# Down stage of a product-key expert layer: which token tiles have their gates scattered, placed by one-hot products, or gathered

## The chip, the cores and the metric

The kernel runs on one core of a Trainium2 chip. The metric is the device time of one launch in microseconds. The core has TensorE (PE), VectorE (DVE), ScalarE (ACT), GpSimd (POOL) and SyncE (SP), each with its own list of instructions that runs in order; they meet in semaphores.

## The reference

One decoder layer over 1024 tokens of width 1024: a mixing sublayer (dilated attention and gated DeltaNet), a norm, a product-key expert sublayer (PEER) and a norm. The change is in PEER:

```python
q = (t @ w_query).reshape(T, PEER_HEADS, 2, PEER_HALF)
s = jnp.einsum('thpc,hpkc->thpk', q, sub_keys).astype(f32)
top_s, top_i = lax.top_k(s, PEER_TOPK)
...
best_s, best_j = lax.top_k(cand_s, PEER_TOPK)
experts = jnp.take_along_axis(cand_i, best_j, axis=-1)
gate = jax.nn.softmax(best_s, axis=-1)
...
act = jax.nn.gelu(jnp.einsum('pd,phkd->phk', xb, expert_down[eb]).astype(f32), approximate=False)
return jnp.einsum('phk,phkd->pd', (gb * act).astype(x.dtype), expert_up[eb])
```

Each token chooses 8 x 16 = 128 of 128 x 128 = 16384 experts, with a gate for each. An expert has one row of `expert_down` and one of `expert_up`.

## The kernel before

Stages run one after the other, with a barrier between: projection, attention, DeltaNet, merge, output projection with norm, scores, then `stage_down_and_route` (the down stage) and `stage_up`.

The 1024 tokens are eight tiles of 128. Six tiles are dense (`DENSE`): the down stage multiplies them with all 16384 experts, in 128 chunks of 128 experts, and stores the gelu as `act`; `stage_up` multiplies `act` by a gate matrix `W` in DRAM, which is zero but for the 128 chosen experts of each token, and by `expert_up`. Two tiles are gathered (`GATHERED`): for them only the chosen rows are read, `expert_down` rows in the down stage and `expert_up` rows in the up stage.

The gates of a dense tile come into `W` in one of two ways. A scattered tile (`SCATTERED`) has its zeroes written in the DeltaNet stage (`blank`, L650) and then has its gates added by 128 indirect DMAs of GpSimd (`scatter`, L1708), one for each choice, of 128 gates each. A placed tile (`PLACED`) has 32 groups of four one-hot products: DVE makes `r_oi` (L1742), ScalarE makes `r_oj` (L1636, L1639), PE multiplies them into `r_psw` (L1923), ScalarE copies that to `r_W` (L1645), and eight DMAs of 1 MB store it (L1587).

Work of the down stage by chunk `c`, each engine in its own loop:

- PE: 48 products of `x1` with the chunk (`L1935`, high and low parts of the weights and of `x1`), two halves of 24. In a chunk that belongs to a placed tile (`pair_in`) two groups of one-hot products follow, one behind each half. A placed tile takes 16 chunks, from four chunks behind its routing; two chunks before them PE transposes its routes (`turn`, L1912).
- ScalarE: gelu of the chunk (`r_act`, L1671) when its products are done, the high part `r_dh` of the weights of chunk `c + 3` (L1618), and its part of the one-hots.
- DVE: the low part `r_dl` of chunk `c + 2` (`split_d`, L1733; three buffers), one-hots, one of the 14 pieces of the routing of a tile (`topk`), the dot products of gathered rows (`dot_row`, L1750), and at the end the one-hots for the first half of chunk `c + 1`. Pieces 12 and 13 are the longest; behind piece 13 the tile is routed. Routed are tiles 0 to 7 in chunks 6, 13, 27, 41, 55, 69, 83 and 97.
- GpSimd: the scatters of the chunk and then the gathers for its dots (L1699): for a dot `k` the row `k + 4` is gathered into the buffer that the dot set free (four buffers, `NGB`). If a group of 16 scatters begins in the chunk, these scatters come behind the gathers, and the first waits for all 16 before.
- SP: loads of weights, stores of `act` and of `W`.

Lists worked out when the kernel is built say how many scatters and dots a chunk has. Before: tile 0's scatters in chunks 7 to 55 (two or three a chunk), tile 4's in 56 to 121 (two), dots in chunks 28 to 83 (two or three) and 84 to 126 (three). Groups of placed tiles are chunks 17 to 32, 45 to 60, 73 to 88 and 101 to 116. All of a kernel's DMAs of GpSimd stand in one list with each other, so a gather waits behind the scatters ahead of it:

```python
for c in range(PK):
    fresh = next((x for x in scatters[c] if x % TOP == 0), scatters[c].stop)
    for x in range(scatters[c].start, fresh):
        scatter(SCATTERED[x // P], x % P)
    if c == first_dots:
        for k in range(NGB):
            gather(k)
    for k in dots[c]:
        if k + NGB < NG2 * P:
            gather(k + NGB)
```

Of the kernel before, what the change touches and what calls it, by code (L numbers as in the profile page):

```python
# [9 lines left out]
ALU = mybir.AluOpType  # L10
# [18 lines left out]
N_BR = 2 * KD  # L29
N_IN = N_ATT + N_DN + N_GB + N_BR  # L30
PH, PK, TOP = 8, 128, 16
SCATTERED = (0, 4)
GATHERED = (2, 6)
PLACED = (1, 3, 5, 7)
DENSE = SCATTERED + PLACED
ORDER = GATHERED + DENSE
ND, NG2 = len(DENSE), len(GATHERED)
# [1435 lines left out]
def stage_down_and_route(nc, g):  # L1473
# [33 lines left out]
        n = stop - first  # L1507
        return [0] * first + [count * (k + 1) // n - count * k // n for k in range(n)]

    split_at = routed_in[SCATTERED[1]] + 1  # L1510
    scatters = spread(evenly(routed_in[SCATTERED[0]] + 1, split_at, P) + evenly(0, PK - 6 - split_at, P))
    scatters += [range(NS * P, NS * P)] * (PK - len(scatters))
    middle = routed_in[GATHERED[1]] + 1
    first_dots = routed_in[GATHERED[0]] + 1
    dots = spread(evenly(first_dots, middle, P) + evenly(0, PK - 1 - middle, P) + [0])
    last_dot = [next(c for c, part in enumerate(dots) if P * (n + 1) - 1 in part) for n in range(NG2)]
    ring = [(k + 1 + k // P) % NGB for k in range(NG2 * P)]
    x_slot = [n * (P + 1) % NGB for n in range(NG2)]
# [8 lines left out]
    with ExitStack() as ctx:  # L1527
        def sb(name, shape, dt=F32):
# [1 line left out]

        sem = ctx.enter_context(stage_semaphores(nc, "r",
            "ld_d0 ld_d1 ld_d2 ld_st ld_c ld_x st_W d_lo gelu st_a0 st_a1 st_used W d_hi shifted exp oi oj off turned rt "
            "d_mm w_mm eq picked summed pieces passed chain zsum routed dots x_in gelu_g coef", landed="ld_g0 ld_g1 ld_g2 ld_g3 put0 put1"))
        xh, xl = g.x1h, g.x1l
        draw = [sb(f"r_draw{u}", [P, KD, P]) for u in range(DEEP)]
        dh = [sb(f"r_dh{u}", [P, KD, P], F32R) for u in range(DEEP)]
# [152 lines left out]
        @block.gpsimd  # L1689
        def _(pool):  # L1690
            def gather(k):
                n, u = k // P, ring[k]
                if k % P == 0:
                    pool.wait_ge(sem("routed"), START + GATHERED[n] + 1)
                if k % P == NGB - 1:
                    pool.wait_ge(sem("x_in"), START + n + 1)
                elif k >= NGB:
                    pool.wait_ge(sem("dots"), START + k - NGB + (2 if 0 <= k - P < NGB - 1 else 1))
                nc.gpsimd.indirect_dma_start(out=rows[u][:], out_offset=None, in_=g.down_rows,  # L1699
                                             in_offset=bass.IndirectOffsetOnAxis(ap=g.ids[:, n, k % P:k % P + 1], axis=0)).then_inc(sem(f"ld_g{u}"), 16)  # L1700

            def scatter(t, e):
                n = SCATTERED.index(t)
                if e == 0:
                    pool.wait_ge(sem("routed"), START + t + 1)
                elif e % TOP == 0:
                    pool.wait_ge(sem(f"put{n}"), 16 * e)
                nc.gpsimd.indirect_dma_start(out=cells, out_offset=bass.IndirectOffsetOnAxis(ap=place[:, n, e:e + 1], axis=0),  # L1708
                                             in_=put[:, n, e:e + 1], in_offset=None, compute_op=ALU.add).then_inc(sem(f"put{n}"), 16)

            cells = g.W.rearrange("j p (t o) -> (j p t) o", o=1)
            for c in range(PK):
# [9 lines that stand above are left out]
                for x in range(fresh, scatters[c].stop):  # L1722
                    scatter(SCATTERED[x // P], x % P)
            for n in range(NS):
                pool.wait_ge(sem(f"put{n}"), 16 * P)

        @block.vector
        def _(dve):
# [33 lines left out]
            def topk(t, piece):  # L1762
# [54 lines left out]
                elif piece == 6:  # L1817
                    before()
                    for h in range(PH):
                        done = nc.vector.max(best[:, h, 0:8], cand[:, h])  # L1820
                elif piece == 7:
                    before()
                    for h in range(PH):
                        done = nc.vector.max_index(flat[:, h, 0:8], best[:, h, 0:8], cand[:, h])
                elif piece == 8:
                    before()
                    for h in range(PH):
                        done = nc.vector.match_replace(out=cand[:, h], in_to_replace=best[:, h, 0:8], in_values=cand[:, h], imm_value=GONE)
                elif piece == 9:
                    before()  # L1830
                    for h in range(PH):
                        done = nc.vector.max(best[:, h, 8:16], cand[:, h])
                elif piece == 10:
                    before()
                    for h in range(PH):
                        nc.vector.max_index(flat[:, h, 8:16], best[:, h, 8:16], cand[:, h])

                    dve.wait_ge(sem("turned"), START + sum(d < t for d in PLACED))
                    nc.vector.tensor_tensor(route[:, 2], best[:], best[:, :, 0:1].broadcast_to([P, PH, TOP]), ALU.subtract).then_inc(sem("shifted"), 1)
                    dve.wait_ge(sem("shifted"), START + t + 1)  # L1840
                    dve.sem_inc(sem("pieces"), 1)
                elif piece == 11:

                    before()
                    nc.vector.tensor_copy(flatf[:], flat[:])
                    chained(nc.vector.scalar_tensor_tensor(comb[:], keyf[:, :, 0, :], 64.0, starts8, ALU.mult, ALU.add), 1)
                    nc.vector.tensor_copy(rise[:, :, 0:1], comb[:, :, 0:1])
                    chained(nc.vector.tensor_tensor(rise[:, :, 1:], comb[:, :, 1:], comb[:, :, 0:TOP - 1], ALU.subtract), 2)
                    dve.wait_ge(sem("exp"), START + t + 1)
                    nc.vector.tensor_reduce(zsum[:], route[:, 2], AX.X, ALU.add).then_inc(sem("zsum"), 1)  # L1850
                    dve.wait_ge(sem("zsum"), START + 2 * t + 1)
                    nc.vector.reciprocal(zsum[:], zsum[:]).then_inc(sem("zsum"), 1)
                    dve.wait_ge(sem("zsum"), START + 2 * t + 2)
                    done = nc.vector.tensor_tensor(route[:, 2], route[:, 2], zsum[:].unsqueeze(2).broadcast_to([P, PH, TOP]), ALU.mult)
                elif piece == 12:
                    before()
                    picked(0, flatf[:], starts16, ALU.is_ge, rise[:])
                    chained(nc.vector.tensor_copy(code[:], route[:, 0]), 3)
                    nc.vector.tensor_scalar(low[:], code[:], 63, None, ALU.bitwise_and)
                    chained(nc.vector.tensor_scalar(high[:], code[:], 6, None, ALU.logical_shift_right), 4)  # L1860
                    nc.vector.tensor_copy(route[:, 0], high[:])
                    chained(nc.vector.tensor_copy(comb[:], low[:]), 5)
                    chained(nc.vector.tensor_tensor(flatf[:], flatf[:], comb[:], ALU.subtract), 6)
                    dve.sem_inc(sem("pieces"), 1)
                elif piece == 13:
                    before()
                    picked(1, flatf[:], ranks16, ALU.is_equal, keyf[:, :, 1, :])
                    if t not in PLACED:
                        both = comb[:].rearrange("p h a -> p (h a)")
                        r0, r1, r2 = (route[:, x].rearrange("p h a -> p (h a)") for x in range(3))  # L1870
                        chained(nc.vector.scalar_tensor_tensor(both, r1, float(PK), r0, ALU.mult, ALU.add), 7)
                        if t in GATHERED:
                            n = GATHERED.index(t)
                            nc.vector.tensor_copy(gate[:, n], r2)
                            chained(nc.vector.tensor_copy(g.ids[:, n], both), 8)
                        else:
                            n = SCATTERED.index(t)
                            nc.vector.tensor_copy(put[:, n], r2)
                            chained(nc.vector.tensor_scalar(place[:, n], both, float(TD), tokens[:, n:n + 1], ALU.mult, ALU.add), 8)
                    else:  # L1880
                        dve.sem_inc(sem("chain"), CHAIN - 6)
                    dve.sem_inc(sem("routed"), 1)  # L1882
                    dve.sem_inc(sem("pieces"), 1)
# [425 lines left out]
```

## Time and profile before

| | us |
|---|---|
| time, median of 3 (4306.22 to 4308.96) | 4306.57 |
| the profiled execution | 4310.81 |
| its span | 4309.0 |
| down stage, first product to last gelu | 1960.0 to 3189.3 |
| up stage, first product | 3208.3 |

| engine | busy us | share of the span |
|---|---|---|
| PE | 3957.7 | 92% |
| DVE | 2586.9 | 60% |
| ScalarE | 1367.3 | 32% |
| GpSimd | 1702.3 | 40% |

Busy times are sums over the whole span and say nothing of one stage. A row of a group gives busy time, the mean ns of one instruction and the idle time of its engine just before, with what ended it. GpSimd is counted busy while it makes the descriptors of an indirect DMA, not while the data move.

### The profile page before, as it was taken

What the parts mean: (1) busy time and instruction counts of PE and PEld (TensorE: products, weight loads), DVE (VectorE), ACT (ScalarE), POOL (GpSimd) and SP (SyncE); (2) the same over time, 40 slices, a digit from 0 to 9 for tenths busy, and PEclk for the clock granted to TensorE, in tenths of its full rate; (3) what the DMA queues carried; (4) which work ended last, traced back from release to release, by engine and by line L of the source; (5) the groups of instructions that cost most, each with busy time, mean ns of one, the idle gap of its engine ahead of it and who ended that gap; (6) DMA issues with size and microseconds to landing.
All of it is one profiled execution on the core that took longest, in us unless ns stands there. A gap on an engine that the chain in (4) does not pass through costs nothing. (4 is left out here: it accounts for less than half of the span.)

```text
span 4309.0 us, 61280 instructions
## 1 busy us (share of the span) xinstructions
PE 3957.7 (92%) x21744; PEld 3573.4 (83%) x21744; DVE 2586.9 (60%) x5114; ACT 1367.3 (32%) x2139; POOL 1702.3 (40%) x1159
## 2 busy tenths in 40 slices
PE   9999994996888788998999999999988999999996
PEld 7888884886888666998999999999976888888885
DVE  2154102554555334116777888886648888898888
ACT  2133221652222211112472644635512222222220
POOL 0000003624444004000727656566626555555556
PEclk9999996997999899999999999999999999999998
DMA  3223224642222322223549779698888888888884
GB/s 132 97 88 106 94 86 129 160 109 71 76 75 84 138 95 94 88 68 129 136 139 318 231 227 299 201 331 278 262 315 289 289 291 290 285 290 298 280 289 185
DMA packets 390923, 801.82 MB, mean 186 GB/s; under 512 B 65265, under 2 KB 204401, under 8 KB 389745
## 3 DMA queue, kind: packets, MB, share of 16 engines
q1 hardware_dynamic: 280176, 531.25, 36.9%
q0 software_dynamic: 110592, 268.62, 19.9%
q8 instruction: 85, 1.39, 0.1%
q14 instruction: 70, 0.57, 0.0%
HBM read 623.40 MB, written 154.32 MB: 180 GB/s over the span
## 5 line engine op out<-in xcount | busy, mean ns | idle before, releaser
L1935 PE MATMUL r_psd<-x1h,r_dh 128*128 128x384 f32 x2048 | 700.9, 342 | 19.0 <-DVE r_dl L1733 19.0
L1935 PE MATMUL r_psd<-x1l,r_dh 128*128 128x384 f32 x2048 | 688.4, 336 | 0.0
L1935 PE MATMUL r_psd<-x1h,r_dl 128*128 128x384 f32 x2048 | 688.3, 336 | 0.0
L2180 PE MATMUL e_psy<-e_uh,e_Ch 128*128 128x512 f32 x1536 | 600.1, 391 | 36.3 <-DVE e_Cl L2105 31.9
L2180 PE MATMUL e_psy<-e_ul,e_Ch 128*128 128x512 f32 x1536 | 599.5, 390 | 0.0
L2180 PE MATMUL e_psy<-e_uh,e_Cl 128*128 128x512 f32 x1536 | 599.4, 390 | 0.0
L1708 POOL DMA_INDIRECT W<-r_put,r_place x256 | 426.7, 1667 | 405.6 <-DVEq L1882 319.0
L2074 POOL TENSOR_TENSOR e_araw<-e_araw,e_W 128x768 f32<-128x768 f32 x128 | 258.9, 2023 | 401.4 <-DMA e_W<-W 400.5
L1935 PEld LDWEIGHTS r_psd<-x1h,r_dh 128*128 128x128 f32 x2048 | 388.3, 190 | 19.8 <-DVE r_dl L1733 19.8
L1699 POOL DMA_INDIRECT r_rows<-in_down_rows,ids x256 | 262.7, 1026 | 358.8 <-DVE coef L1750 242.8
L2130 DVE SCALAR_TENSOR_TENSOR e_y<-e_rows,coef,e_y 128x1024 f32<-128x1024 f32 x256 | 384.5, 1503 | 15.0 <-DMA e_rows<-in_up,ids 14.9
L1935 PEld LDWEIGHTS r_psd<-x1l,r_dh 128*128 128x128 f32 x2048 | 388.3, 190 | 0.0
L1935 PEld LDWEIGHTS r_psd<-x1h,r_dl 128*128 128x128 f32 x2048 | 387.4, 189 | 0.0
L2052 ACT CAST e_uh<-e_uraw 128x1024 fp32r<-128x1024 f32 x128 | 134.8, 1053 | 789.8 <-DMA e_uraw<-in_up 495.8
L244 PE MATMUL p_ps<-p_xh,p_wh 128*128 128x512 f32 x928 | 362.0, 390 | 10.3 <-DVE p_wl L198 10.1
L2180 PEld LDWEIGHTS e_psy<-e_uh,e_Ch 128*128 128x128 f32 x1536 | 289.7, 189 | 97.8 <-DVE e_Cl L2105 32.7
L244 PE MATMUL p_ps<-p_xl,p_wh 128*128 128x512 f32 x928 | 361.6, 390 | 0.0
L244 PE MATMUL p_ps<-p_xh,p_wl 128*128 128x512 f32 x928 | 361.5, 390 | 0.0
L2068 POOL DMA_INDIRECT e_rows<-in_up,ids x256 | 331.2, 1294 | 59.1 <-issue 45.2
L2180 PEld LDWEIGHTS e_psy<-e_uh,e_Cl 128*128 128x128 f32 x1536 | 289.5, 188 | 60.5
L2180 PEld LDWEIGHTS e_psy<-e_ul,e_Ch 128*128 128x128 f32 x1536 | 289.7, 189 | 60.1
L1750 DVE CUSTOM_DVE_ANT_0 r_rows<-r_rows,r_psx 128x1024 f32<-128x1024 f32 x256 | 301.2, 1214 | 42.5 <-DMA r_rows<-in_down_rows,ids 37.1
(326 smaller groups left out, 7338.3 us busy)
## 6 DMA issues: line engine op xcount, KB each, us to landing
r_draw<-in_down SPq DMA_DIRECT2D x128, 512.0 KB, 5.3
e_uraw<-in_up SPq DMA_DIRECT2D x128, 512.0 KB, 6.2
act<-r_act SPq DMA_DIRECT2D x128, 384.0 KB, 5.0
e_araw<-act SPq DMA_DIRECT2D x128, 384.0 KB, 3.2
e_W<-W SPq DMA_DIRECT2D x128, 384.0 KB, 5.0
W<-r_W SPq DMA_DIRECT2D x32, 1024.0 KB
p_wraw<-in_w_in SPq DMA_DIRECT2D x58, 512.0 KB, 3.7
hT<-p_out SPq DMA_DIRECT2D x58, 512.0 KB, 2.9
```

The source lines that it names most:

```text
L244: ins = nc.tensor.matmul(ps[u][:, h * HALF:(h + 1) * HALF], a[u][:, k, :], b[:, k, h * HALF:(h + 1) * HALF], start=(k == 0 and n == 0), st ...
L1699: nc.gpsimd.indirect_dma_start(out=rows[u][:], out_offset=None, in_=g.down_rows, in_offset=bass.IndirectOffsetOnAxis(ap=g.ids[:, n, k % P: ...
L1708: nc.gpsimd.indirect_dma_start(out=cells, out_offset=bass.IndirectOffsetOnAxis(ap=place[:, n, e:e + 1], axis=0), in_=put[:, n, e:e + 1], i ...
L1750: nc.vector.tensor_tensor_reduce(out=rows[u][:], in0=rows[u][:], in1=psx[:], scale=1.0, scalar=0.0, op0=ALU.mult, op1=ALU.add, accum_out=d ...
L1935: ins = nc.tensor.matmul(psd[n][:, h, 0:HD], a[c % DEEP][:, k, :], b[:, k, h * HD:(h + 1) * HD], start=(k == 0 and m == 0), stop=(k == KD ...
L2052: nc.scalar.copy(uh[s][:], uraw[n][:]).then_inc(sem("u_hi"), 1)
L2068: nc.gpsimd.indirect_dma_start(out=rows[u][:], out_offset=None, in_=g.up.rearrange("j p d -> (j p) d"), in_offset=bass.IndirectOffsetOnAxi ...
L2074: nc.gpsimd.tensor_tensor(araw[n][:], araw[n][:], Wt[n][:], ALU.mult).then_inc(sem("weighted"), 1)
L2130: nc.vector.scalar_tensor_tensor(o, rows[u][:], scale, o, ALU.mult, ALU.add).then_inc(sem("acc"), 1)
L2180: ins = nc.tensor.matmul(bank[:], a[s][:, t * P:(t + 1) * P], v[s][:, h * HALF:(h + 1) * HALF], start=(q == 0 and m == 0), stop=(q == G - ...
```

## The change

Three tiles are scattered (0, 3, 6) and three are placed (1, 4, 7); 2 and 5 are gathered. The lists change with them. Tile 0's scatters are five a chunk from chunk 7 (to 32), tile 3's 3.2 a chunk from 42 (to 81), tile 6's 3.4 a chunk from 84 (to 121). Dots are three or four a chunk in 28 to 41, then 2.4 a chunk to 126. Groups of placed tiles are chunks 17 to 32, 59 to 74 and 101 to 116. In chunk 28, where the first gathers are, its five scatters stand ahead of them. `put` and `place` keep two buffers for three scattered tiles, so tile 6's routing waits until tile 0's scatters have landed. Through `NS`, `TS` and `ORDER` the zeroed part of `W` grows from 256 to 384 tokens, and the order of the tiles in `x1h`, `g.s` and the up stage follows.

```diff
@@ -29,9 +29,9 @@
-SCATTERED = (0, 4)
-GATHERED = (2, 6)
-PLACED = (1, 3, 5, 7)
+SCATTERED = (0, 3, 6)
+GATHERED = (2, 5)
+PLACED = (1, 4, 7)
@@ -1507,12 +1507,22 @@
-    split_at = routed_in[SCATTERED[1]] + 1
-    scatters = spread(evenly(routed_in[SCATTERED[0]] + 1, split_at, P) + evenly(0, PK - 6 - split_at, P))
-    scatters += [range(NS * P, NS * P)] * (PK - len(scatters))
+    starts_at = [routed_in[t] + 1 for t in SCATTERED]
+    first_gathers = routed_in[GATHERED[0]] + 1
+    counts = [0] * PK
+    for t, first in zip(SCATTERED, starts_at):
+        rate = 5 if first < first_gathers else 3.2 if t != SCATTERED[-1] else 3.4
+        for k in range(P):
+            counts[first + int(k / rate)] += 1
+    scatters = spread(counts)
     middle = routed_in[GATHERED[1]] + 1
     first_dots = routed_in[GATHERED[0]] + 1
-    dots = spread(evenly(first_dots, middle, P) + evenly(0, PK - 1 - middle, P) + [0])
+    early = (starts_at[1] - first_dots) * 7 // 2
+    late = PK - 1 - starts_at[1]
+    dots = [0] * first_dots + [3 + n % 2 for n in range(starts_at[1] - first_dots)]
+    early = sum(dots)
+    dots += [(NG2 * P - early) * (n + 1) // late - (NG2 * P - early) * n // late for n in range(late)] + [0]
+    dots = spread(dots)
@@ -1705,8 +1715,8 @@
-                nc.gpsimd.indirect_dma_start(out=cells, out_offset=bass.IndirectOffsetOnAxis(ap=place[:, n, e:e + 1], axis=0),
-                                             in_=put[:, n, e:e + 1], in_offset=None, compute_op=ALU.add).then_inc(sem(f"put{n}"), 16)
+                nc.gpsimd.indirect_dma_start(out=cells, out_offset=bass.IndirectOffsetOnAxis(ap=place[:, n % 2, e:e + 1], axis=0),
+                                             in_=put[:, n % 2, e:e + 1], in_offset=None, compute_op=ALU.add).then_inc(sem(f"put{n}"), 16)
@@ -1875,8 +1885,10 @@
-                            nc.vector.tensor_copy(put[:, n], r2)
-                            chained(nc.vector.tensor_scalar(place[:, n], both, float(TD), tokens[:, n:n + 1], ALU.mult, ALU.add), 8)
+                            if n >= 2:
+                                dve.wait_ge(sem(f"put{n - 2}"), 16 * P)
+                            nc.vector.tensor_copy(put[:, n % 2], r2)
+                            chained(nc.vector.tensor_scalar(place[:, n % 2], both, float(TD), tokens[:, n:n + 1], ALU.mult, ALU.add), 8)
```

The rest of the diff adds the semaphore `put2`.

## Rows read from the trace of the kernel before

**Rows 1.** The page, busy time of each engine.

```profile
PE 3957.7 (92%) x21744; PEld 3573.4 (83%) x21744; DVE 2586.9 (60%) x5114; ACT 1367.3 (32%) x2139; POOL 1702.3 (40%) x1159
```

**Rows 2.** One tile's instructions, `r_act`, seven stretches: count, ns min/median/max, first and last start.

```profile
L1671 ACT ACTIVATE r_act<-r_psd x11: 814/815/816, 2278.3 to 2361.5; 128x768 f32<-128x768 f32 x11
L1671 ACT ACTIVATE r_act<-r_psd x9: 811/811/812, 2136.1 to 2217.0; 128x768 f32<-128x768 f32 x9
L1671 ACT ACTIVATE r_act<-r_psd x17: 811/811/815, 2105.3 to 2269.1; 128x768 f32<-128x768 f32 x17
L1671 ACT ACTIVATE r_act<-r_psd x17: 811/811/816, 2370.2 to 2548.7; 128x768 f32<-128x768 f32 x17
L1671 ACT ACTIVATE r_act<-r_psd x17: 811/811/815, 2649.8 to 2825.2; 128x768 f32<-128x768 f32 x17
L1671 ACT ACTIVATE r_act<-r_psd x17: 811/811/815, 2926.3 to 3096.9; 128x768 f32<-128x768 f32 x17
L1671 ACT ACTIVATE r_act<-r_psd x12: 811/815/815, 3096.9 to 3189.3; 128x768 f32<-128x768 f32 x12
```

**Rows 3.** The timeline of PE at chunk 45; busy times by stretch (PEclk: granted clock).

```profile
2379.97 2.08 PE L1923 MATMUL r_psw<-r_oj,r_oi 128*128 128x128 f32 x8 [5.65 <-DVE r_oi L1742]
2387.79 1.05 PE L1923 MATMUL r_psw<-r_oj,r_oi 128*128 128x128 f32 x8
...
2378.80:2385.60 6.80, 5.63 (x20) 5.64 (x21) 6.80 (x28) 2.75 (x6) 5.58 (x5) 0.50 0.85 265
```

**Rows 4.** DMA issues: KB each, median us from issue to landing.

```profile
W<-r_W SPq DMA_DIRECT2D x32, 1024.0 KB
W<-d_none SPq DMA_DIRECT2D x8, 2048.0 KB, 9.1
r_rows<-in_down_rows,ids POOLq DMA_INDIRECT x256, 6.4
```

**Rows 5.** Groups on GpSimd, stretches 2036:2154.4, 2221:3190 (two) and 2826:2926.

```profile
L1708 POOL DMA_INDIRECT W<-r_put,r_place x57 | 92.2, 1618 | 345.0 <-DVEq L1882 319.0 <-issue 16.2 <-DMA W<-r_put,r_place 9.9
...
L1708 POOL DMA_INDIRECT W<-r_put,r_place x199 | 334.5, 1681 | 60.6 <-issue 60.6
L1699 POOL DMA_INDIRECT r_rows<-in_down_rows,ids x256 | 262.7, 1026 | 358.8 <-DVE coef L1750 242.8 <-DVEq L1882 67.2 <-issue 48.8
...
L1708 POOL DMA_INDIRECT W<-r_put,r_place x20 | 35.3, 1763 | 6.1 <-issue 6.1
```

**Rows 6.** The timeline of GpSimd and of DVE around the first gather.

```profile
2221.54 1.01 POOL L1699 DMA_INDIRECT r_rows<-in_down_rows,ids  x1 [67.23 <-DVEq L1882]
2222.86 1.69 POOL L1699 DMA_INDIRECT r_rows<-in_down_rows,ids  x1 [0.30 <-issue]
...
2230.86 1.22 DVE L1750 CUSTOM_DVE_ANT_0 r_rows<-r_rows,r_psx 128x1024 f32<-128x1024 f32 x1 [1.89 <-DMA r_rows<-in_down_rows,ids]
```

**Rows 7.** Waits: DVE's in the stage, then GpSimd's, 2470:2508, 2608:2650, 2756:2795; a row of DVE.

```profile
DVE r_rows L1750 <- DMA r_rows<-in_down_rows,ids: 37.1, 26, 5.4
...
POOL r_rows L1699 <- DVE coef L1750: 19.8, 3, 8.0
...
POOL r_rows L1699 <- DVE coef L1750: 14.9, 3, 9.2
...
POOL r_rows L1699 <- DVE coef L1750: 20.6, 3, 13.7
...
L1777 DVE TENSOR_REDUCE r_route<-r_pick 128x64 f32<-128x1024 f32 x32 | 39.0, 1220 | 1.1
```

**Rows 8.** One tile's instructions, `r_put` and `r_rows`; busy times by stretch.

```profile
L1708 POOL DMA_INDIRECT W<-r_put,r_place x256: 1536/1576/2549, 2036.1 to 3133.3; - x128
...
L1699 POOL DMA_INDIRECT r_rows<-in_down_rows,ids x256: 935/967/1987, 2221.5 to 3170.0; - x128
...
2036.10:2152.80 116.70, 115.62 (x690) 114.74 (x690) 95.50 (x440) 52.17 (x89) 90.67 (x57) 1.00 0.60 134
```

More of the change, by code:

```diff
@@ L1532, in stage_down_and_route @@
             "ld_d0 ld_d1 ld_d2 ld_st ld_c ld_x st_W d_lo gelu st_a0 st_a1 st_used W d_hi shifted exp oi oj off turned rt "
-            "d_mm w_mm eq picked summed pieces passed chain zsum routed dots x_in gelu_g coef", landed="ld_g0 ld_g1 ld_g2 ld_g3 put0 put1"))
+            "d_mm w_mm eq picked summed pieces passed chain zsum routed dots x_in gelu_g coef", landed="ld_g0 ld_g1 ld_g2 ld_g3 put0 put1 put2"))
         xh, xl = g.x1h, g.x1l
```

## Prediction

> **What bounds the kernel now.** I read the busy times first: PE works 92% of the span, GpSimd 40% [rows 1]. An average over stages can't tell what the change is worth, so I went to the down stage, chunk by chunk. The gelu of a chunk (L1671) starts when its PE work is done, so its starts give the pitch. Without one-hot products ten pitches take 2361.5 - 2278.3 = 83.2 us, 8.32 us a chunk. In a group of a placed tile eight take 2217.0 - 2136.1 = 80.9 us, 10.11 us, so a chunk's one-hot products cost 1.79 us. A placed tile has 16 such chunks. From the gelu before a group to its last gelu the four groups take 163.8, 178.5, 175.4 and 170.6 us; with 0.8 us because the last gelu lies ahead of the last products, and less 16 x 10.11 = 161.8, PE stood or ran slowly for 2.8, 17.5, 14.4 and 9.6 us [rows 2]. What it stood for is DVE's one-hots: 5.65 us at chunk 45. Then the granted clock was at half (0.50 for 6.8 us, the lower level, 1.2 GHz), and eight products took 2.08 us and not 1.05; PE worked 5.63 us of that stretch, half of which, 2.8, is lost [rows 3]. So before, PE sets the pace and DVE adds short stalls. The question is whether GpSimd, at work beside them, can still be left out.
>
> **What goes.** Tile 3 is no longer placed: 16 x 1.79 = 28.6 us of products and 0.4 us of transposes leave PE. One group's stalls go with it; the groups of tiles 1 and 7 keep their chunks, the group of tile 4 (chunks 59 to 74) stands to its routing as that of tile 5 stood, so the 17.5 us of tile 3's group go. Together -46.5 us, if nothing else binds. ScalarE's copies and DVE's one-hots of the tile go too, both beside PE. Eight stores of 1 MB go from the down stage; eight zeroing stores in the DeltaNet stage grow from 2 to 3 MB. They land in 9.1 us and are issued behind the loads of their chunk [rows 4]; half as much again is 4.6 us each in a chunk pitch of some 46 us, so 0, at worst 8 x 4.6 = 37 if each were in the way of a load, which nothing shows. Two routings get three small DVE instructions instead of none; the new wait on put0 at tile 6 asks for scatters over long before (chunk 83 against 32): 0.
>
> **What comes: 128 scatters on GpSimd, and where they stand in its queue.** Its list is in order: scatters of a chunk, then the gathers of its dots. A scatter takes 1.62 us and 0.30 us to the next while GpSimd scatters alone, 1.68 + 0.30 = 1.98 among gathers; a gather 1.03 + 0.30 = 1.33. The first of each 16 waits for those before, 9.9 us in three waits [rows 5].
>
> *Chunks 7 to 32.* Tile 0 now has 5 scatters a chunk; that is 5 x 1.92 = 9.6 us against 8.32. Before, GpSimd had done its 57 scatters by 2154.3 and stood 67.2 us until the first gather, at 2221.54, which waited only for the routing of tile 2. Now 110 scatters stand ahead of it. The 57th, which ended at 2154.3, was issued at 2152.8; 54 more pitches of 1.92 and three waits of 3.3 make 2266. The gather is 45 us late. DVE has the first dots in its list in chunk 28 and was waiting for rows even before (1.89 us) [rows 6]; behind them stand the one-hots for chunk 29, so PE stands at chunk 29 for these 45 us. One more dot (1.1), the half clock (2.8) and the rest of tile 0 come on top: in chunks 29 to 31 GpSimd has 15 scatters and 11 gathers, 44.3 us against 30.4, of which about 9 reach PE. Together 45 + 1.1 + 2.8 + 9 = +58.
>
> *From the first gather to the end* GpSimd has 18 + 256 scatters and 256 gathers: 274 x 1.98 + 256 x 1.33 = 883 us. By chunk: 42 to 58 carry 55 scatters and 41 gathers, 163 us against 17 x 8.32 = 141; 84 to 100 carry 58 and 41, 169 against 141. In the groups it just fits (153 and 160 against 162). GpSimd can't use the free chunks ahead of time, as a scatter waits for its tile's routing and a gather for the dot four before. So free time is lost: chunks 33 to 41 hold 32 gathers and no scatter, 74.9 - 42.6 = 32 us; 82 and 83: 10; the two groups: 9 + 2; 122 to the end: 37. That is 90 us. And it waits for dots where DVE does the last two pieces of a routing, twelve instructions of 1.22 us and small ones, 17 us with no dot between but two or three: at three such places before 19.8, 14.9 and 20.6 us [rows 7]. After, there are five; at two (54, 96) GpSimd is so late that it isn't the one who waits, so 3 x 15 = 45. The end of the stage's work is then 2266 + 883 + 90 + 45 = 3284, where the last gelu was at 3189.3 and the end 0.9 later [rows 2]: +94. From PE's side I get nearly the same. The stretch of chunks 42 to 58 with the start of its group costs 22 + 15 of waits, the one of 84 to 100 costs 28 + 20; two or three half clocks of 2.8 each make 43 and 56, and I put what DVE's lead takes up at 5 each: 38 + 51. Of these 9.6 (start of tile 7's group) and about half of tile 5's 14.4 were there before. -46.5 + 58 + 89 - 17 = +84. I take +90, between the two.
>
> Ends of the unknown: nothing lost in waits and each operation at its median (1.58 and 0.97, [rows 8], 1.27 with the gap) make 274 x 1.88 + 256 x 1.27 = 840 and an end at 3196, +6, but DVE's pieces do cost waits. With durations halfway to the medians (1.93 and 1.30, 862 us) and half of the 45 the end is 3240, +50; the low end of my range, +34, lies between. Upward, in the densest bare stretch scatters took 1.76 [rows 5]: 274 x 0.08 = 22 more, and rows that land in 8 and not 6.4 us [rows 4] keep DVE and GpSimd waiting for each other, some 20 more: +130.
>
> **A rule against it.** The scatters ran beside a DVE at work 95.5 of 116.7 us and took 1.54 at least, 1.58 in the median and 2.55 at most [rows 8]. The Trainium skill, page "SBUF — State Buffer", section "SBUF: two separate sides", says that a DVE operation in a two-port mode locks GpSimd out of the port it writes descriptors by, and that a DMA of some 620 ns alone took some 3100 beside one. By that factor a scatter would take 7.7 us and 128 of them some 770 us more, by the rows 128 x 1.98 = 253 us of GpSimd's time. The trace doesn't show the lock at that size; that sentence and its sum change nothing here.
>
> **The rivals.**
> - *PE goes on setting the pace* (5 in 100): DVE's lead and the ring of four rows hide GpSimd's 22 and 28 us, and the scatters of tile 0 run faster than 1.62. Then 4306.6 - 46.5 = 4260. For it: GpSimd is only 40% busy over the span [rows 1], PE's group work does go. Against it: 110 scatters in the 185 us from 2036.1 [rows 8] to the gather's 2221.5 would need 1.69 us each with the gap; the fastest takes 1.54 + 0.30 = 1.84. It decides for faster only if the hole at chunk 29 is under 47 us and nothing is lost later.
> - *Only the hole at chunk 29 counts* (6 in 100): -46.5 + 58 = +11.5, 4318. DVE may be two chunks behind PE (three buffers of split weights), 15 us, and that would have to take the 22 and the 28. Against it: the lead has to be given back where a group begins, as 9.6 us at tile 7's [rows 2].
> - *More than that* (11 in 100): scatters at 1.76 and slow landings, +130, 4437.
> - *The forecast* (78 in 100): +90.
>
> **How the numbers follow.** The profiled execution took 4310.8 (span 4309.0), 4.2 over the median 4306.6. With +90 a profiled one would be 4401, and the median 4396. The range of the forecast, +34 to +130, is 4340 to 4437; with the upper rival's better half to 4445 it holds 8 in 10. 0.2% (8.6 us) is what a measurement of this kernel can tell from no change. Faster: 0.05, the first rival. Within it: 0.03, half of the second. Slower: 0.92.
>
> **What would show it.** The first gather of the stage near 2266 and PE idle for 40 us and more near 2233, released by DVE's one-hot (L1742). DVE idle for landings of rows (L1750) some 250 us in all, or more, instead of 37 [rows 7]. PE stalls on r_dl (L1733) in the bare chunks 46 to 58 and 84 to 100, which before had none. Groups of tiles 4 and 7 that start with 10 us and more of idle PE. GpSimd busy close to 1100 us with its gaps, and the stage 90 us longer; all other stages as they were. Wrong would be: a first gather before 2240, pitches of 8.32 in chunks 84 to 100, or a change outside the stage.

## The result, and the profile after

| | before | after |
|---|---|---|
| median of the runs | 4306.4 us | 4413.12 us (4407.03 to 4421.29) |
| profiled execution | 4310.81 us | 4407.03 us |
| its span | 4309.0 us | 4405.2 us |
| first to last gelu of the down stage | 1216.7 us | 1315.5 us |

The ratio is 1.0249 with a 95% interval of 1.023 to 1.0268: 107 us slower by the medians, 96 in the profiled executions. The down stage carries all of it: +98.8 us between its first and last gelu, +1.7 ahead of it and -4.3 behind it. Lines of the changed kernel stand 10 to 12 lower (the scatter is L1718, the gather L1709, the dot L1760, `r_dl` L1743, `r_oi` L1752, the one-hot products L1935, the gelu L1681).

The page of the changed kernel, engines and the dearest group:

```profile
PE 3957.0 (90%) x21485; PEld 3565.3 (81%) x21485; DVE 2555.6 (58%) x4989; ACT 1277.2 (29%) x1946; POOL 1916.9 (44%) x1287
...
L1718 POOL DMA_INDIRECT W<-r_put,r_place x384 | 629.5, 1639 | 453.8 <-DVEq L1894 318.3
```

GpSimd's share rises only from 40% to 44% [rows 1], and PE's busy sum doesn't fall, as products at the half clock count as busy for longer: the same 6144 products of `x1` took 708.4 + 695.9 + 695.6 = 2099.9 us for 2077.6 before. These rows alone would not show what happened.

The gelu by stretch, as in [rows 2]: the groups of tiles 1, 4 and 7 (first to last start over 16 chunks), then the gelus of chunks 42 to 58, of 83 to 100, and of the end:

```profile
L1681 ACT ACTIVATE r_act<-r_psd x17: 811/811/816, 2106.9 to 2326.4; 128x768 f32<-128x768 f32 x17
L1681 ACT ACTIVATE r_act<-r_psd x17: 811/811/815, 2577.7 to 2762.4; 128x768 f32<-128x768 f32 x17
L1681 ACT ACTIVATE r_act<-r_psd x17: 811/811/816, 3020.3 to 3197.4; 128x768 f32<-128x768 f32 x17
...
L1681 ACT ACTIVATE r_act<-r_psd x17: 811/813/817, 2416.0 to 2577.7; 128x768 f32<-128x768 f32 x17
L1681 ACT ACTIVATE r_act<-r_psd x18: 811/811/816, 2838.2 to 3020.3; 128x768 f32<-128x768 f32 x18
...
L1681 ACT ACTIVATE r_act<-r_psd x12: 811/815/815, 3197.4 to 3289.8; 128x768 f32<-128x768 f32 x12
```

With 161.8 us for 16 chunks and 0.8 for the shift, the three groups lose 58.5, 23.7 and 16.1 us. Between the first group and the second, 26 chunks of 8.32 us are 216.3, with the same 0.8 217.1, and take 2577.7 - 2326.4 = 251.3: 34.2 lost. Chunks 84 to 100 take 182.1 us for 141.4: 40.7 lost. Chunks 75 to 83 lose nothing (2838.2 - 2762.4 = 75.8 for 74.9 + 0.8), nor does the end. The sum is 173.2 us, where the kernel before lost 44.3; less the 29 us of PE work that went, that is +99.9, the 98.8 of the table.

The timeline (start, us of one, engine, instruction, idle before it and what ended it) of GpSimd around the first gather of the stage, of DVE at the first dot and of PE at chunk 29:

```profile
2265.27 1.54 POOL L1718 DMA_INDIRECT W<-r_put,r_place  x1 [0.30 <-issue]
2267.12 1.01 POOL L1709 DMA_INDIRECT r_rows<-in_down_rows,ids  x1 [0.31 <-issue]
```

```profile
2271.56 1.22 DVE L1760 CUSTOM_DVE_ANT_0 r_rows<-r_rows,r_psx 128x1024 f32<-128x1024 f32 x1 [42.20 <-issue]
```

```profile
2278.25 2.08 PE L1935 MATMUL r_psw<-r_oj,r_oi 128*128 128x128 f32 x8 [43.69 <-DVE r_oi L1752]
```

Against [rows 6]: the gather no longer waits for the routing (67.23 us idle before) but comes 0.3 us behind a scatter, 45.6 us later. DVE stands until 4.4 us behind that gather (the profile names no releaser for its 42.20 us; it is the first dot, and it needs the row), PE for the one-hot that stands behind the dots in DVE's list, and its next products run at the half clock (2.08 us for eight).

Waits in the down stage (total, count, longest), and behind them GpSimd's groups from the first gather to the end (busy time, ns of one | idle before):

```profile
DVE r_rows L1760 <- DMA r_rows<-in_down_rows,ids: 229.7, 76, 12.9
...
POOL r_rows L1709 <- DVE coef L1760: 138.0, 79, 9.8
...
PE r_psw L1935 <- DVE r_oi L1752: 83.7, 9, 43.7
```

```profile
L1718 POOL DMA_INDIRECT W<-r_put,r_place x274 | 450.7, 1645 | 85.1 <-issue 82.0 <-DMA W<-r_put,r_place 3.2
L1709 POOL DMA_INDIRECT r_rows<-in_down_rows,ids x256 | 274.6, 1073 | 192.9 <-DVE coef L1760 138.0 <-issue 54.9
```

DVE's wait for rows was 37.1 us [rows 7], and PE waited for weights (`r_psd` on `r_dl`) only at the start of the stage. Now, in chunks 87 to 100:

```profile
DVE r_rows L1760 <- DMA r_rows<-in_down_rows,ids: 49.2, 11, 7.7
...
PE r_psd L1947 <- DVE r_dl L1743: 18.0, 8, 4.0
...
POOL r_rows L1709 <- DVE coef L1760: 8.1, 10, 3.7
```

These are PE's stalls of 4 us and less, eight of them in 152 us. In the 20 us ahead of each of the longer ones DVE had waited 4 to 12 us for rows. The rows were not slow to land: where a dot waited, it began 6.8 us (median of 75) behind the start of its gather, and 7.7 us before the change (26). Nor were the DMA engines fuller, in a bare stretch after and before (the last three numbers are granted clock, DMA share, GB/s):

```profile
2838.00:3020.00 182.00, 155.35 (x822) 151.70 (x821) 129.90 (x349) 36.66 (x48) 131.37 (x94) 0.93 0.80 218
```

```profile
2826.00:2926.00 100.00, 100.00 (x580) 99.96 (x580) 76.63 (x174) 28.22 (x39) 68.47 (x53) 1.00 1.06 351
```

So the gathers were issued late.

### The profile page after: what moved, and what is told of

Same layout as the page of the kernel before. It is cut to its first block and busy times, and to the rows that moved or that the text cites. A ratio compares the mean times of both kernels' runs of the same rounds, so it can differ in the third digit from the quotient of the medians.

```text
span 4405.2 us, 60496 instructions
## 1 busy us (share of the span) xinstructions
PE 3957.0 (90%) x21485; PEld 3565.3 (81%) x21485; DVE 2555.6 (58%) x4989; ACT 1277.2 (29%) x1946; POOL 1916.9 (44%) x1287
## 5 line engine op out<-in xcount | busy, mean ns | idle before, releaser
L1718 POOL DMA_INDIRECT W<-r_put,r_place x384 | 629.5, 1639 | 453.8 <-DVEq L1894 318.3
L1947 PE MATMUL r_psd<-x1h,r_dh 128*128 128x384 f32 x2048 | 708.4, 346 | 67.9 <-DVE r_dl L1743 66.9
L1947 PE MATMUL r_psd<-x1l,r_dh 128*128 128x384 f32 x2048 | 695.9, 340 | 0.0
L1947 PE MATMUL r_psd<-x1h,r_dl 128*128 128x384 f32 x2048 | 695.6, 340 | 0.0
L1760 DVE CUSTOM_DVE_ANT_0 r_rows<-r_rows,r_psx 128x1024 f32<-128x1024 f32 x256 | 305.3, 1216 | 281.5 <-DMA r_rows<-in_down_rows,ids 229.7
L2142 DVE SCALAR_TENSOR_TENSOR e_y<-e_rows,coef,e_y 128x1024 f32<-128x1024 f32 x256 | 390.9, 1528 | 14.3 <-DMA e_rows<-in_up,ids 14.2
L1709 POOL DMA_INDIRECT r_rows<-in_down_rows,ids x256 | 274.6, 1073 | 192.9 <-DVE coef L1760 138.0
L309 POOL TENSOR_TENSOR a_raw<-a_raw,a_cos 128x1024 f32<-128x1024 f32 x11 | 27.1, 2468 | 746.3 <-DMA a_raw<-hT 746.3
## 6 DMA issues: line engine op xcount, KB each, us to landing
W<-d_none SPq DMA_DIRECT2D x8, 3072.0 KB, 11.6
```

The lines of the kernel that those rows point to most:

```text
L309: engine.tensor_tensor(raw[n][:], raw[n][:], (cos, sin)[n % 2][:], ALU.mult).then_inc(turned, 1)
L1760: nc.vector.tensor_tensor_reduce(out=rows[u][:], in0=rows[u][:], in1=psx[:], scale=1.0, scalar=0.0, op0=ALU.mult, op1=ALU.add, accum_out=d ...
L1947: ins = nc.tensor.matmul(psd[n][:, h, 0:HD], a[c % DEEP][:, k, :], b[:, k, h * HD:(h + 1) * HD], start=(k == 0 and m == 0), stop=(k == KD ...
L2142: nc.vector.scalar_tensor_tensor(o, rows[u][:], scale, o, ALU.mult, ALU.add).then_inc(sem("acc"), 1)
```

## The experiments

The theory: GpSimd's one list sets the pace, through rows that reach DVE late (A). Rivals: the loss is not GpSimd's list, which stays hidden (B), full DMA engines (C), the hole at chunk 29 alone (D). Where a text below gives what some chunks lose, it is the time from PE's first product of the first chunk to that of the chunk behind the last, less 8.32 us for each chunk, or 10.11 with one-hot products.

**e1, the kernel before with tile 0's scatters at five a chunk.**

```diff
+    counts = [len(part) for part in scatters]
+    counts[routed_in[SCATTERED[0]] + 1:split_at] = [0] * (split_at - routed_in[SCATTERED[0]] - 1)
+    for k in range(P):
+        counts[routed_in[SCATTERED[0]] + 1 + k // 5] += 1
+    scatters = spread(counts)
```

> The kernel before (tiles 0 and 4 scattered, four placed), and only the rate of tile 0's scatters as in the changed kernel: five a chunk from chunk 7 instead of two or three. Nothing else of the change. Theory A (GpSimd's list is in order, 110 scatters stand ahead of the first gather): first gather at about 2266, one hole of PE of about 45 us at chunk 29, a half clock after it, and 5 to 9 us for the last 18 scatters: 4306 + 50 to 60, about 4361. Theory B (PE sets the pace and the order of GpSimd's list is hidden behind DVE's lead): within 10 us of 4306.

4353.07 us, ratio 1.0109 (1.0092 to 1.0126), which is +47 (+44 against the median of the runs beside it, 4309.46). Its first gather and PE's stall, from the timelines of the two engines:

```profile
2264.35 1.01 POOL L1704 DMA_INDIRECT r_rows<-in_down_rows,ids  x1 [0.30 <-issue]
```

```profile
2273.66 2.08 PE L1928 MATMUL r_psw<-r_oj,r_oi 128*128 128x128 f32 x8 [41.81 <-DVE r_oi L1747]
```

The gather and the hole are as A said, with none of the change's third tile. The total is some 8 us under A's 4361: chunks 17 to 32 lose 47.3 us for 2.9 before, which is the hole of 41.8 and some 2.6 at the half clock, and every other stretch loses within 0.2 us what it lost before. Of the 5 to 9 us that I had put down for the last 18 scatters nothing shows.

**e2, the kernel before with the early dots.**

```diff
-    dots = spread(evenly(first_dots, middle, P) + evenly(0, PK - 1 - middle, P) + [0])
+    dots = [0] * first_dots + [3 + n % 2 for n in range(42 - first_dots)]
+    dots += evenly(0, middle - 42, P - sum(dots)) + evenly(0, PK - 1 - middle, P) + [0]
+    dots = spread(dots)
```

> The kernel before, and only its dots in chunks 28 to 41 at three or four a chunk as in the changed kernel (49 there instead of 32), fewer in 42 to 83. It tells what the faster gathers beside the stores of W of tile 1 (chunks 33 to 40) cost by themselves. Theory A (GpSimd's time alone): 2.6 scatters and 3.5 gathers are 9.8 us a chunk against 8.32, 13 us over nine chunks, mostly within DVE's lead: 0 to +8. Theory C (the DMA engines are full in chunks 33 to 43, so ScalarE waits for stores and weights): PE stands for weights near chunk 43 also here, +8 to +20.

4324.49 us, ratio 1.0042 (1.0028 to 1.0056), +18 (+15 against the runs beside it): over A's number, inside C's. Chunks 33 to 44 lose 15.8 us for 0.4. A wait of ScalarE in 2325 to 2375 us, and PE's timeline:

```profile
ACT r_act L1673 <- DMA act<-r_act: 20.1, 3, 10.0
```

```profile
2366.43 0.69 PE L1937 MATMUL r_psd<-x1h,r_dh 128*128 128x384 f32 x1 [7.13 <-DVE r_dl L1735]
```

Both readings were open: ScalarE waits for stores, and PE for DVE. e6 tells them apart.

**e3, the changed kernel with every second scatter of tiles 3 and 6 left out.**

```diff
+                if n > 0 and e % 2:
+                    return
...
-                    pool.wait_ge(sem(f"put{n}"), 16 * e)
+                    pool.wait_ge(sem(f"put{n}"), 16 * e if n == 0 else 8 * e)
```

> The changed kernel; of the scatters of tiles 3 and 6 every second one is left out (their gates are not added), so GpSimd has 128 scatters fewer, spread over chunks 42 to 121; tile 0 as it is. Theory A: 1.6 scatters and 2.4 gathers are 6.4 us a chunk against 8.32, PE sets the pace from chunk 42 on. Only the hole at chunk 29 is left: 4306 - 46 + 58 = 4318, and up to 15 more if the loss at chunk 43 has another cause. Theory B (the loss behind chunk 42 is not GpSimd's list, but the order of tiles, DVE or the DMA engines): above 4380, as the changed kernel.

4328.88 us, ratio 1.0047 (1.0030 to 1.0064): 84 us come back with 128 scatters. DVE's and PE's waits from 2421 us to the end of the stage:

```profile
DVE r_rows L1762 <- DMA r_rows<-in_down_rows,ids: 58.7, 22, 8.1
...
PE r_psd L1949 <- DVE r_dl L1745: 4.4, 1, 4.4
```

In the changed kernel the same two, over 2421 to 3290, are:

```profile
DVE r_rows L1760 <- DMA r_rows<-in_down_rows,ids: 204.2, 57, 12.9
...
PE r_psd L1947 <- DVE r_dl L1743: 48.0, 20, 5.0
```

So what is lost behind chunk 42 hangs on the number of scatters; B falls. With half of them gone nearly all of that loss is gone: chunks 84 to 100 lose 0.5 us, and 38.9 in the changed kernel.

**e4, the changed kernel with tile 0's scatters at 4.25 a chunk.**

```diff
-            counts[first + int(k / rate)] += 1
+            if first < first_gathers:
+                counts[first + int(k / 4.25) if k < 89 else first_gathers + int((k - 89) / 2.9)] += 1
+            else:
+                counts[first + int(k / rate)] += 1
```

> The changed kernel; tile 0's scatters at 4.25 a chunk in chunks 7 to 27 (89 of them) and 2.9 a chunk in 28 to 41 (39), so that the first gather isn't behind them. Theory A (what counts is GpSimd's whole load): the gather is 45 us earlier, but 21 more scatters, 42 us, come behind it, into chunks that had 32 us free: -35, about 4378. Theory D (only the hole counts): -58 and no more lost, about 4355.

4382.71 us, ratio 1.0178 (1.0161 to 1.0195): -30. PE's stall at chunk 29:

```profile
2250.45 2.07 PE L1938 MATMUL r_psw<-r_oj,r_oi 128*128 128x128 f32 x8 [9.76 <-DVE r_oi L1755]
```

The stall there shrinks by 34 us, from 43.69 to 9.76, and 30 arrive at the end; the gather was still 17 us late (2238.6), so it isn't the clean case that I expected. Part of what is moved comes back as load, as A has it: chunks 17 to 32 lose 42 us less than in the changed kernel, and chunks 33 to 74 16 us more. D's 4355 is excluded.

**e5, the changed kernel with one scatter in 128.**

```diff
+                if e > 0:
+                    return
```

> The changed kernel with nearly all scatters left out: of each scattered tile only the first of 128 is issued (the gates of tiles 0, 3 and 6 are otherwise not added). It is the change's gain alone: one tile fewer in one-hot products. Theory A (everything lost is GpSimd's list): 4307 - 46 = 4260 where nothing else is new, and 4260 + 8 to 15 = 4268 to 4275 with the loss near chunk 43 that the early dots brought (e2). Theory B (the order of tiles, the larger zeroing or the new wait cost too): above 4290.

4262.63 us, ratio 0.9899 (0.9882 to 0.9915): the gain that PE's side promised, 4260, is there as soon as GpSimd's list has no scatters. The larger zeroing and the new order of the tiles cost nothing that shows. The new wait is not tested by it, as here it asks for one landing and not for 128; in the trace of the changed kernel DVE never waits for a landing of `W`.

**e6, e2 with thin stores of tile 1's gates.**

```diff
-TS = NS * P
+TS = (NS + 1) * P
...
+                if t == PLACED[0]:
+                    w = 1
```

> As e2 (the kernel before with three or four dots a chunk in 28 to 41), but the stores of W of tile 1 are cut from 1 MB to 64 KB each (the rest of its gates is not stored; the zeroing in the DeltaNet stage covers its columns instead, 3 MB and not 2). Theory C (what e2 lost is DMA engines that are full of the 512-byte rows of W beside more gathers): the 15 us come back, 4306 to 4312. Theory E (it is GpSimd's list, 9.8 us a chunk against 8.32): it stays at 4320 to 4326.

4321.98 us, ratio 1.0037 (1.0023 to 1.0051). ScalarE's waits for stores are gone from 2325 to 2375 us, and PE's stall is not:

```profile
2367.51 0.69 PE L1939 MATMUL r_psd<-x1h,r_dh 128*128 128x384 f32 x1 [6.84 <-DVE r_dl L1737]
```

So in e2 it is not the stores, and C falls for it. E's number holds. That DVE's own list of early dots and two long pieces doesn't make the stall by itself is seen in e10, which has the same list and thin stores but no scatters: there chunks 42 to 58 lose 0.8 us in all.

**e7, the kernel before with later groups.**

```diff
-        first = max(routed_in[t] + 4, free)
+        first = {1: 17, 3: 50, 5: 78, 7: 104}[t]
```

> The kernel before, with the chunks of one-hot products of tiles 3, 5 and 7 begun at 50, 78 and 104 instead of 45, 73 and 101, farther behind the two long routing pieces. Theory A (a group that begins while DVE is 8 to 12 us behind makes PE give back DVE's lag and pay a half clock; later the lag is gone): 8.5 of tile 3's stalls, 5.5 of tile 5's and 9.5 of tile 7's go, -20 or so: 4286. Rival (the stall only moves, as the one-hots then add to DVE's list elsewhere): within 5 us of 4307.

4317.33 us, ratio 1.0017 (1.0006 to 1.0028): no gain, but some 7 us lost. The stall at the start of tile 5's group is gone (3.78 us at chunk 73 before), those of the other two grew, from 5.65 us at chunk 45 to 11.36 at 50 and from 7.32 at 101 to 11.94 at 104. PE at chunk 104, and DVE ahead of it, at two of its twelve waits for rows in 2920 to 2968 us:

```profile
2968.07 2.07 PE L1924 MATMUL r_psw<-r_oj,r_oi 128*128 128x128 f32 x8 [11.94 <-DVE r_oi L1743]
```

```profile
2927.77 1.22 DVE L1751 CUSTOM_DVE_ANT_0 r_rows<-r_rows,r_psx 128x1024 f32<-128x1024 f32 x1 [4.35 <-DMA r_rows<-in_down_rows,ids]
2964.61 1.22 DVE L1751 CUSTOM_DVE_ANT_0 r_rows<-r_rows,r_psx 128x1024 f32<-128x1024 f32 x1 [4.57 <-DMA r_rows<-in_down_rows,ids]
```

My expectation was wrong: seven chunks behind the routing DVE's lag is still there. The reading that e8 tests is that two scatters and three gathers are 8 us a chunk, so that rows come late also in the kernel before.

**e8 and e9, the scatters laid where GpSimd has time**, with the groups of e7 (e8) and with the old groups (e9, whose list differs from chunk 33 on).

```diff
+    counts = [0] * PK
+    for first, stop, n in ((7, 28, 4), (28, 33, 2), (33, 50, 1), (50, 55, 3), (55, 56, 2), (56, 66, 3),
+                           (66, 78, 1), (78, 94, 3), (94, 104, 1), (104, 118, 2)):
+        counts[first:stop] = [n] * (stop - first)
+    scatters = spread(counts)
```

> As e7 (the kernel before, groups of tiles 3, 5 and 7 at 50, 78 and 104), and the scatters of tiles 0 and 4 laid where GpSimd has time: four a chunk in 7 to 27 (84, before the first gather), one a chunk where chunks hold no one-hot products, two or three where they do. Theory A (in e7 DVE's lag stayed because GpSimd had 8 us of work in a chunk of 8.3 and handed the rows late): the stalls at 50, 78 and 104 go, 4307 - 15 to 20, 4287 to 4292. Rival (DVE's own list keeps the lag): as e7, 4312 to 4320.

> The kernel before with its groups where they were (17, 45, 73, 101), and only the scatters laid as in e8: four a chunk in 7 to 27, one a chunk without one-hot products, two or three with them. Theory A: tile 7's group at 101 begins without GpSimd's share of the lag, -5 to -9; tiles 3 and 5 begin four chunks behind long routing pieces and keep their stalls: 4298 to 4302. Rival (scatters cost nothing in the kernel before): within 3 us of 4307.

e8 takes 4298.53 us, ratio 0.9982 (0.9973 to 0.9991) over 11 runs: it beats the kernel before by some 8 us, and e7, from which only the places of the scatters part it, by 19. The stall at chunk 50 is gone, and the group of tile 3 loses 8.9 us for e7's 22.7 and 17.6 before; the stall at 104 has halved, 6.02 us for 11.94:

```profile
2946.99 2.07 PE L1929 MATMUL r_psw<-r_oj,r_oi 128*128 128x128 f32 x8 [6.02 <-DVE r_oi L1748]
```

It is the fastest version that computes the whole layer, though short of the 15 to 20 that I expected. e9 takes 4305.06, ratio 0.9996 (0.9987 to 1.0005): the rival's number, and 4298 to 4302 was missed. The placing of scatters alone is worth nothing measurable; with the later groups it is.

**e10, e5 with thin stores of tile 1's gates.**

```diff
-TS = NS * P
+TS = (NS + 1) * P
...
+                if t == PLACED[0]:
+                    w = 1
```

> As e5 (one scatter of 128 for each scattered tile, gates otherwise not added), and the stores of W of tile 1 cut from 1 MB to 64 KB each (the rest is not stored; the zeroing covers its columns, 4 MB and not 3). Theory C (near chunk 43 ScalarE waits for stores of act that land late, 33.8 us in e5, because the 512-byte rows of W and 3.5 gathers a chunk fill the DMA engines): these waits go, chunk 43 takes 8.3 us and not 12.9: 4262 - 5 = 4257, and less if it had cost elsewhere. Rival (DVE's own list in chunks 40 to 43, two long routing pieces and seven dots, makes the stall): chunk 43 stays near 13 us, 4260 to 4264.

Chunk 43 did as C says. In e5, a gelu of ScalarE near chunk 43, PE at the first product of chunk 44, and ScalarE's wait for stores over the whole span:

```profile
2370.22 0.81 ACT L1681 ACTIVATE r_act<-r_psd 128x768 f32<-128x768 f32 x1 [6.15 <-DMA act<-r_act]
```

```profile
2371.08 0.45 PE L1949 MATMUL r_psd<-x1h,r_dh 128*128 128x384 f32 x1 [4.47 <-DVE r_dl L1745]
```

```profile
ACT r_act L1681 <- DMA act<-r_act: 33.8, 5, 10.5
```

In e10 there is no such wait and no such stall, DVE no longer waits for the high part `r_dh` that ScalarE makes behind its gelu (4.0 us in 2320 to 2372 us of e5), PE's pitch at chunk 43 falls from 12.95 to 8.64 us, and the stage from its first to its last gelu takes 1166.5 us instead of 1171.9. But the kernel took 4281.08 us and not 4257, 18 more than e5: all ahead of the down stage, whose first gelu came at 1994.9 and not at 1973.9. The time is lost where the zeroes are written: from the first piece to the last 346 us pass and not 325, and PE there waits 17.1 us in six waits for loads (`d_raw`) instead of 2.1 in three. The piece of 4 MB:

```profile
W<-d_none SPq DMA_DIRECT2D x8, 4096.0 KB, 14.2
```

## Why the prediction was right

- *First gather at 2266, PE idle for 45 us at chunk 29.* Measured 2267.1 and 43.7 us; the group of tile 1 lost 58.5 where it had lost 2.8, +55.7 for the +58 of the sum. e1 has nearly the same hole (41.8) from the rate alone.
- *The gain of PE's side, -46.5.* e5 has the sum, 4262.6 against 4260, but not term by term. The products of a tile and tile 3's stalls went, and tile 4's group lost 15.7 us in e5 where tile 5's had lost 14.5, as forecast. But without scatters tile 7's group loses 0.1 and not 9.6, and chunks 17 to 32 and 42 to 58 lose 3.7 and 6.4 us more; that these offset each other is luck.
- *GpSimd's account after the first gather.* 883 us of operations were forecast; 450.7 + 82.0 + 274.6 + 54.9 = 862 came. 135 us of waits and tail were forecast; 138.0 + 3.2 + 19.6 (last gather to last gelu) = 161 came. That the two errors nearly cancel is luck: 3284 forecast, 3289.8 measured. The mean scatter was 1.65 and not 1.68 us. Of the waits, those in chunks 33 to 41 were 31.5 us (forecast 32), behind the routings of tiles 3, 5 and 6 57.7 (45), from chunk 122 to the end 33.7 with the tail (37); the other 38 us stand where 21 were forecast, in many short waits.
- *The stretches.* 42 to 58 and 84 to 100 lose 34.2 (with 33 to 41) and 40.7; with the starts of their groups they carry the rest of the loss, and none is lost in 75 to 83 or behind 117, as forecast. With their groups that is 57.9 + 56.8 = 115 us where 38 + 51 = 89 were forecast, so the sum from PE's side, +84, was 15 us short of the stage's 98.8; the forecast of +90 was put between it and GpSimd's +94. DVE's waits for rows were forecast at 250 or more; 229.7 are so labelled, and the 42.2 of the hole come on top.
- *What the scatters cost, by chunk.* The changed kernel against e5, which has three of them: 51.1 us in chunks 17 to 32, 28.1 in 42 to 58, 8.1 in 59 to 74, 38.5 in 84 to 100 and 16.2 in 101 to 116. Two thirds of what tile 4's group loses are there without them.
- *What was missed.* I took GpSimd's time as the bound. In chunks 87 to 100 GpSimd, with its gaps, works 145 of 152 us, but over the stage it also waits 138 us for DVE: the two wait for each other over a ring of four rows, and neither is full. And near chunk 43 part of the loss is ScalarE waiting for stores: the changed kernel stalls there for 5.0 us, as e5 does for 4.5, and in e10 that goes with the stores. It is some 5 us of the 107.
- The zeroing stores stood 54 us apart and not 46, and cost nothing, as forecast.
- The forecast was +90 against +107 by the medians, +96 in the profiled execution. The rivals "PE goes on setting the pace" and "only the hole counts" would have been e5's and about e3's time; the load of tiles 3 and 6 on GpSimd is what parts them from the measured one.

With 384 scatters beside a busy DVE a scatter took 1.64 us in the mean and 2.81 at most, where the mean before was 1.67 and the longest 2.55 [rows 8]. The lock of GpSimd's port beside DVE, which the Trainium skill tells of (page "SBUF — State Buffer", section "SBUF: two separate sides"), is not borne out here at the factor of five of its example. Which of DVE's instructions here would take that lock was not tried.

## What to carry to other kernels

An engine that is 40% busy over the span can be nearly full in the stretch where work is added (145 of 152 us here): count its operations per chunk with their gaps, and look at what stands behind them in its list. Here 0.3 us between operations and an order fixed at build time turned a cheap scatter into a late gather, and the late gather reached PE through DVE. Where two engines pass rows through a small ring, relieve the chunks in which the bound engine runs fastest, and move the consumer's critical work with it: here the later groups alone lost some 7 us (e7), the moved scatters alone won nothing (e9), both together won 8 us (e8).

## What the runs showed that I had not expected

- Zeroing `W` in eight pieces of 2, 3 and 4 MB (landing in 9.1, 11.6 and 14.2 us) began the down stage at 1960.0, 1961.7 and 1982.3 us. Over all profiles the start lies at 1958.9 to 1965.8 with 2 MB and at 1961.7 to 1968.9 with 3 MB: the third megabyte costs next to nothing, the fourth some 20 us in the one profile that has it, where PE waits for loads. Why there is a step was not tried.
- In e7 a later group start made PE's stall longer (11.94 us at chunk 104 for 7.32 at chunk 101 before). The reading is that DVE's lag doesn't decay while rows come late; e8, with fewer scatters ahead of the same start, has 6.02 us.
